# Latents, recurrence queries, first output and the queries of two head pairs turned by VectorE in 32x32 blocks and through DRAM

## The reference

```
h = rms_norm(x);  p = h @ W_in            # columns: hq hf hi hg (1024 each), c_q 512, c_kv 512, k_rope 64
o_A: 8 heads, gated linear recurrence:    # q = silu(hq), f = lb + (1-lb) sigmoid(hf), k = 1-f, v = hi
     S_t = diag(f_t) S_(t-1) + k_t v_t^T,  o_t = S_t^T q_t;  o_A = rms_norm(o) * silu(hg)
o_B: 8 heads, latent attention:           # q = rms_norm(c_q) @ w_uq,  k, v = rms_norm(c_kv) @ w_ukv
     head norms and rotary tail on q and k, softmax over chunks of 64 up to the query's, times v
x = x + concat(o_A, o_B) @ W_out
x = x + (silu(gate) * up) @ w_down        # gate, up = rms_norm(x) @ w_gate_up, width 5632
```

## Time and profile before

| | |
|---|---|
| median of 3 runs | 1124.82 us (1124.74 to 1125.54) |
| the profiled execution's own time | 1124.67 us |
| its span, first to last instruction | 1122.9 us |
| TensorE matmuls busy | 1113.2 us, 99% |
| VectorE busy | 886.8 us, 79% |
| ScalarE busy | 640.5 us, 57% |
| GpSimd busy | 51.1 us, 5% |
| moved by DMA | 228.99 MB, mean 204 GB/s |
| granted clock | 1.00 |

### The profile page before, as it was taken

How to read it: one execution, slowest core, us unless ns; L and a number is a source line. 1 busy time by engine, 2 the same in 40 slices (tenths; PEclk the granted TensorE clock), 3 DMA queues, 4 the chain that set the end, 5 groups by cost and what they waited for, 6 DMA issues and landing times.

```text
span 1122.9 us, 15465 instructions
## 1 busy us (share of the span) xinstructions
PE 1113.2 (99%) x5265; PEld 937.8 (84%) x5265; DVE 886.8 (79%) x1198; ACT 640.5 (57%) x907; POOL 51.1 (5%) x134
## 2 busy tenths in 40 slices
PE   7999999999999999999999999999999999999998
PEld 7988888888888888888888888888888888888887
DVE  5578786587876667688888888888988879889777
ACT  7566776668664556454554554554554555555553
POOL 3000000000000000000000000000000010000000
PEclk9999999999999999999999999999999999999999
DMA  8666455545555455667777677777777686666655
GB/s 267 192 196 189 158 159 156 164 141 170 197 177 168 153 187 169 212 212 234 225 229 237 222 232 238 222 229 236 224 235 226 224 276 217 207 206 199 211 190 169
DMA packets 107239, 228.99 MB, mean 204 GB/s; under 512 B 8201, under 2 KB 19250, under 8 KB 106930
## 3 DMA queue, kind: packets, MB, share of 16 engines
q1 hardware_dynamic: 101346, 209.30, 58.9%
q0 software_dynamic: 5536, 18.88, 5.8%
q10 hardware_dynamic: 304, 0.14, 0.0%
HBM read 218.32 MB, written 9.96 MB: 203 GB/s over the span
## 4 chain that ended last, share of the span: by engine, by line
PE 97%; DVE 2%; DMA 1%; ACT 0%; issue 0%; SPq 0%; DVEq 0%; ACTq 0%
PE side L1919 25%; PE main L1693 22%; PE side L1921 12%; PE main L1696 11%; PE side L1891 4%; PE side L1892 4%; PE side L1893 4%; PE main L1893 3%; PE main L1891 3%; PE main L1892 3%; PE side L1817 1%; PE side L1716 1%; DMA raw<-in_w_in 1%; PE side L1764 0%; PE side L1765 0%; DVE w_lo L1084 0%
## 5 line engine op out<-in xcount | busy, mean ns | idle before, releaser
L977 ACT CAST w_hi<-raw 128x1024 fp32r<-128x1024 f32 (+1 forms) x245 | 241.6, 990 | 172.2 <-PE side L1919 104.9
L1532 DVE TENSOR_TENSOR w_lo<-raw,w_hi 128x1024 fp32r<-128x1024 f32 (+1 forms) x245 | 275.4, 1139 | 21.9 <-ACT w_hi L977 21.6
L1084 DVE TENSOR_TENSOR w_lo<-raw,w_hi 128x1024 fp32r<-128x1024 f32 (+3 forms) x156 | 178.5, 1154 | 107.9 <-ACT w_hi L757 105.6
L757 ACT CAST w_hi<-raw 128x1024 fp32r<-128x1024 f32 (+3 forms) x156 | 153.7, 993 | 142.5 <-PE main L1693 137.6
L1693 PE MATMUL main<-w_hi,hT_hi 128*128 128x512 f32 (+2 forms) x448 | 173.4, 388 | 1.7 <-DVE hT_lo L1105 1.4
L1696 PE MATMUL main<-w_hi,hT_lo 128*128 128x512 f32 (+2 forms) x448 | 169.1, 378 | 0.0
L1921 PE MATMUL side<-w_hi,hT_lo 128*128 128x512 f32 x400 | 155.6, 389 | 0.0
L1919 PE MATMUL side<-w_hi,hT_hi 128*128 128x512 f32 x400 | 155.6, 389 | 0.0
L1693 PE MATMUL main<-w_lo,hT_hi 128*128 128x512 f32 (+2 forms) x448 | 114.6, 377 | 0.0
L1919 PE MATMUL side<-w_lo,hT_hi 128*128 128x512 f32 x400 | 106.9, 389 | 0.0
L1693 PEld LDWEIGHTS main<-w_hi,hT_hi 128*128 128x128 f32 x448 | 84.7, 189 | 15.5 <-DVE hT_lo L1105 1.8
(11 more groups left out here) (279 smaller groups left out, 1819.0 us busy)
## 6 DMA issues: line engine op xcount, KB each, us to landing
raw<-in_w_gate_up SPq DMA_DIRECT2D x176, 512.0 KB, 4.8
raw<-in_w_down SPq DMA_DIRECT2D x88, 512.0 KB, 4.5
raw<-in_w_in SPq DMA_DIRECT2D x64, 512.0 KB, 3.8
raw<-in_w_out SPq DMA_DIRECT2D x32, 512.0 KB, 3.7
raw<-in_w_in SPq DMA_DIRECT2D x15, 384.0 KB, 4.5
squares<-hiddenT POOLq DMA_DIRECT2D x11, 512.0 KB, 5.0
hiddenT<-squares POOLq DMA_DIRECT2D x44, 128.0 KB, 5.3
raw<-in_w_ukv SPq DMA_DIRECT2D x8, 512.0 KB, 3.9
```

The lines of the kernel that those rows point to most:

```text
L757: copy(w_hi[:, slot, 0:n], raw[:, slot, 0:n]).then_inc(s_hi, 1)
L977: copy(w_hi[:, n % RING, 0:cols], src).then_inc(s_hi, 1)
L1084: tt(w_lo[:, slot, 0:n], raw[:, slot, 0:n], w_hi[:, slot, 0:n].bitcast(F32), ALU.subtract)\
L1532: tt(w_lo[:, n % RING, 0:cols], src, w_hi[:, n % RING, 0:cols].bitcast(F32), ALU.subtract)\
```

## The change

Latents 0 and 1, the recurrence's queries of both halves, the first half's output, and the attention's queries of head pairs 0 and 1 are no longer turned by TensorE. A new step `swap` has VectorE transpose the tile in 32x32 blocks into a buffer; GpSimd writes that to a new DRAM tensor `swapped`, waits until it is there, and reads it back in four pieces; the steps `lat_t`, `turn` g 0, `o_t` 0 and `q_t` 0 and 1 remain, without TensorE's part, and take their values from the buffer in SBUF. Buffers are tiles that are idle at that time, and two new ones.

The positions: `swap` of the latents 19 and 27, of hq 34 and 74, of q 36 and 56, of the first output 81. `lat_t` goes from 22 (both) to 30 and 31, and from 30 (both) to 36 and 37; `q_t` 0 and 1 from 39 and 59 to 47 and 67; `turn` 0 0 stays at 45, `turn` 1 0 goes from 89 to 83; `turn` g 1 and `o_t` 0 (95) stay. On VectorE `swap` q j comes behind `q_b` j, `swap` hq 0 behind `kr_b`, `swap` hq 1 behind `q_b` 2, and `swap` o behind `o_b` 0.

```diff
+MOVED_HEADS = 2
 def schedule():
     for i in range(2):
         e = END[("lat", i + 1)]
-        s += [(e + 1, ("lat_a", i)), (e + 2, ("lat_b", i))] + [(e + 5, ("lat_t", i, n)) for n in range(2)]
+        s += [(e + 1, ("lat_a", i)), (e + 2, ("lat_b", i)), (e + 2, ("swap", "lat", i))]
+        s += [(e + 13 - 2 * i + n, ("lat_t", i, n)) for n in range(2)]
...
-        s += [(q - early, ("q_a", j)), (q - 1 if early else q + 1, ("q_b", j)), (q + 4, ("q_t", j))]
+        s += [(q - early, ("q_a", j)), (q - 1 if early else q + 1, ("q_b", j))]
+        s += [(q + 1, ("swap", "q", j)), (q + 12, ("q_t", j))] if j < MOVED_HEADS else [(q + 4, ("q_t", j))]
...
-        s += [(e + 2 + 2 * g + n * (1 + g), ("turn", g, n, t)) for n in range(2) for t in range(NT)]
+        s += [(END[("hq", g)] + 1, ("swap", "hq", g))]
+        s += [(e + 2 - 4 * g, ("turn", g, 0, t)) for t in range(NT)] + [(e + 3 + 3 * g, ("turn", g, 1, t)) for t in range(NT)]
...
-        s += [(p, ("o_a", g)), (p + 1, ("o_b", g))]
+        s += [(p, ("o_a", g)), (p + 1, ("o_b", g))] + [(p + 1, ("swap", "o", g))] * (g == 0)
...
+        hq_turned = mb("hq_turned", [P, P // Q, SEQ])
+        heads = mb("heads", [P, P // Q, NT * 2 * Q + NT * Q])
+        swap_of = {("lat", 0): hbT[:, :, :], ("lat", 1): hkT[:, :, :], ("o", 0): hgate.rearrange("p t (a c) -> p (t a) c", a=2)}
+        for j in range(MOVED_HEADS):
+            swap_of[("q", j)] = heads[:, :, :]
+        swap_of[("hq", 0)] = E[:, 0, :].rearrange("p (a c) -> p a c", a=P // Q)
+        swap_of[("hq", 1)] = hq_turned[:, :, :]
...
+            def swap(*key):
+                n, at = SWAP[key], swap_of[key]
+                wide = at.shape[2]
+                pool.wait_ge(s_swap, n + 1)
+                pool.dma_start(swapped[n, :, :, :, 0:wide].rearrange("a c b x -> (a c) b x"), at).then_inc(s_parked, 16)
+                pool.wait_ge(s_parked, 16 * (n + 1))
+                for b in range(P // Q):
+                    pool.dma_start(at[Q * b:Q * (b + 1), :, :], swapped[n, :, :, b, 0:wide].rearrange("a c x -> c a x"))\
+                        .then_inc(s_landed, 16)
+            swap("lat", 0)
+            swap("lat", 1)
+            swap("hq", 0)
+            for j in range(MOVED_HEADS):
+                swap("q", j)
             pool.wait_ge(s_lbused, 1)
             pool.wait_ge(s_side, USE[("join8", 0)] + 1)
             pool.dma_start(lb[:, :, :], hgrn_lb[:, GW:2 * GW].partition_broadcast(P)).then_inc(s_lbin, 16)
+            swap("hq", 1)
+            swap("o", 0)
...
+            def landed(*key):
+                act.wait_ge(s_landed, MOVED * (SWAP[key] + 1))
                 elif kind == "lat_t":
-                    split_hi([(mT_hi[:, k + n, :], ps[:, n * SEQ:(n + 1) * SEQ], col + n) for n in range(2)])
+                    landed("lat", i)
+                    split_hi([(by_quarter(mT_hi[:, k + n, :]), swapped_tile(("lat", i), 2 * j + n), col + n)
+                              for n in range(2)])
                 elif kind in ("q_t", "k_t"):
+                    if kind == "q_t" and j < MOVED_HEADS:
+                        landed(*key)
+                        for h in range(2):
+                            copy(by_quarter(plain[:, 2 * j + h, :]), straight[:, :, h, :, :])
+                        for h in range(2):
+                            part = slice(h * ROPE, (h + 1) * ROPE)
+                            ins = copy(by_quarter(qTr[part, j % 2, h, :]), turned[part, :, :, :])
+                        ins.then_inc(s_heads, 1)
+                        return
...
-                dve.wait_ge(s_tlo, SPLIT[s] + 1)
-                dve.sem_inc(s_given["dve"], 1)
+                if side_uses(s):
+                    dve.wait_ge(s_tlo, SPLIT[s] + 1)
+                    dve.sem_inc(s_given["dve"], 1)
+            def swap(key, src):
+                nc.vector.transpose(swap_of[key].rearrange("p b (n r) -> p n b r", r=Q),
+                                    src.rearrange("p t (k b c) -> p (t k) b c", b=P // Q, c=Q)).then_inc(s_swap, 1)
                 elif kind == "lat_t":
-                    split_lo(s, [(mT_lo[:, k + n, :], ps[:, n * SEQ:(n + 1) * SEQ], mT_hi[:, k + n, :], col + n)
-                                 for n in range(2)])
+                    split_lo(s, [(by_quarter(mT_lo[:, k + n, :])[:, t, :, :], swapped_tile(("lat", i), 2 * j + n)[:, t, :, :],
+                                  by_quarter(mT_hi[:, k + n, :])[:, t, :, :], col + n) for n in range(2) for t in range(NT)])
+                elif kind == "swap":
...
+                    elif what == "q":
+                        dve.wait_ge(s_stage, 2 * i + 1)
+                        if i:
+                            dve.wait_ge(s_heads, i)
...
+                    elif what == "hq":
+                        b = BLOCK_OF[a]
+                        dve.wait_ge(s_taken[b % 2], taken(b))
+                        swap(a, hq[:, :, :])
+                    else:
+                        dve.wait_ge(s_given["dve"], GIVEN[USE[("o_a", i, NT - 1)]])
+                        swap(a, E[:, 0, :].rearrange("p (t c) -> p t c", t=NT))
...
-                elif kind == "lat_t":
-                    i, j = a
-                    pe.wait_ge(s_lat, NT * (i + 1))
-                    turn_x(s, 2 * j, latents[i])
-                elif kind in ("q_t", "k_t"):
+                elif kind == "k_t" or kind == "q_t" and a[0] >= MOVED_HEADS:
...
                 elif kind == "scores":
                     given(("k_t", h // 2, 1))
+                    if h // 2 < MOVED_HEADS:
+                        pe.wait_ge(s_heads, h // 2 + 1)
...
-                elif kind == "turn":
+                elif kind == "turn" and a[1]:
...
-                elif kind == "o_t":
+                elif kind == "o_t" and a[0]:
```

More of the change, by code:

```diff
@@ L327 @@
 SPLIT = {step: n for n, step in enumerate(SPLITS)}
+SWAPS = [step[1:] for _, step in SCHEDULE if step[0] == "swap"]
+SWAP = {key: n for n, key in enumerate(SWAPS)}
 RMS = [step for _, step in SCHEDULE if step[0] in ("r1a", "lat_a", "q_a", "k_a", "o_a", "r2a")]
@@ L891, in step @@
                                "hg": (hgate, ACT.Silu)}[kind]
-                    if kind == "hq" and not a[0]:
-                        act.wait_ge(s_side, USE[("lat_t", 0, 1)] + 1)
+                    if kind == "hq":
+                        act.wait_ge(s_swap, SWAP[("hq", 0) if a[0] else ("lat", 0)] + 1)
                     if a[0] and kind == "hg":
-                        act.wait_ge(s_given["dve"], GIVEN[USE[("o_a", 0, NT - 1)]])
+                        act.wait_ge(s_tlo, SPLIT[("o_t", 0, 1)] + 1)
                     for t in range(NT):
@@ L902, in step @@
                         act.wait_ge(s_join, g)
-                    src = filled(s)[:, :].rearrange("p (h t) -> p h t", h=GH)
                     if n == 0:
-                        copy(hqT[:, :, t * P:(t + 1) * P], src).then_inc(s_given["act"], 1)
-                    else:
+                        landed("hq", g)
+                        src = swap_of[("hq", g)].rearrange("p a (t h r) -> p t h a r", t=NT, r=Q)[:, t, :, :, :]
+                        copy(hqT[:, :, t * P:(t + 1) * P].rearrange("p h (a r) -> p h a r", r=Q), src)
+                    else:
+                        src = filled(s)[:, :].rearrange("p (h t) -> p h t", h=GH)
+                        if not g and t == 0:
+                            act.wait_ge(s_tlo, SPLIT[("lat_t", 1, 1)] + 1)
                         activation(hkT[:, :, t * P:(t + 1) * P], src, ACT.Copy, scale=-1.0, bias=1.0)
@@ L946, in step @@
                     g, j = a
-                    dst, k = (hT_hi, 12 + 2 * j) if g else (mT_hi, MT[HEADS + 2 * j])
-                    split_hi([(dst[:, k:k + 2, :], filled(s)[:, :].rearrange("p (k t) -> p k t", k=2), V_HG)])
+                    if not g:
+                        landed("o", g)
+                        split_hi([(by_quarter(mT_hi[:, MT[HEADS + 2 * j + n], :]), swapped_tile(("o", g), 2 * j + n), V_HG)
+                                  for n in range(2)])
+                        return
+                    k = 12 + 2 * j
+                    split_hi([(hT_hi[:, k:k + 2, :], filled(s)[:, :].rearrange("p (k t) -> p k t", k=2), V_HG)])
                 elif kind == "sq2":
@@ L1246, in step @@
                     reciprocal((kind[0] + "_a",) + a, inv[:, 0:4], 4)
-                    if j:
+                    if kind == "q_b" and 0 < j <= MOVED_HEADS:
+                        dve.wait_ge(s_swap, SWAP[("q", j - 1)] + 1)
+                    elif j:
                         dve.wait_ge(s_side, USE[(kind[0] + "_t", j - 1, 1)] + 1)
@@ L1408, in step @@
                     g, j = a
-                    hi, lo, k = (hT_hi, hT_lo, 12 + 2 * j) if g else (mT_hi, mT_lo, MT[HEADS + 2 * j])
-                    split_lo(s, [(lo[:, k:k + 2, :], filled(s)[:, :].rearrange("p (k t) -> p k t", k=2),
-                                  hi[:, k:k + 2, :], V_HG)])
+                    if not g:
```

(18 more changed lines are left out.)

33 lines of the change are left out of this document (27 added, 6 removed).

## The result

Five runs of the changed kernel took 1130.85 us in the median (1130.01 to 1131.42), five of the kernel before 1124.82 (1124.74 to 1125.54): a ratio of 1.0051, with a 95% interval of 1.0039 to 1.0064. The change costs 6 us where I had forecast none. The profiled execution of the changed kernel took 1131.42 us, its span is 1129.2.

The account below looks back on a forecast made before the run. TensorE, busy 1113.2 of 1122.9 us, was taken to bound the kernel. The terms -5.7 +0.7 +0.3 +2.0 +1.1 +1.2 gave -0.4 us, a forecast of 1124.4 us, range 1121.0 to 1127.8.

Parts of the forecast that it names:

- Stages 36 to 42: 0.3 us: VectorE's added work makes low halves late at granules 40 and 42: 0.2 and 0.1 us, bounds 0 and 1.5.
- Stages 43 to 52: 2.0 us: First pairs: query copies make ScalarE's chain 1.1 us later, TensorE reaches the wait 0.87 earlier; 2.0 us, bounds 1.0 and 2.8.
- Landings cost nothing: Moves through DRAM: landings cost nothing unless they take 1.5 times what they take later in this kernel.
- It is wrong if ScalarE waits for weights: Sign against the forecast: ScalarE waiting for weights or landings; no wait of ScalarE for DMA was expected.
- The rival of the slow weight loads: Transfers slow the weight loads, weighed between granules 78 and 82: 0.6 us for each of seven moves, 1128.6 us; chance 0.10.
- Stages 31 to 33: 0.7 us: TensorE waits before granule 33 for the first latents' late second split: 0.7 us, bounds 0.2 and 1.4.
- Stages 74 to 88: 1.1 and 1.2 us: Block transposes at 74 and 81 delay the first output's product by 1.1 us in all and granule 88 by 1.2.
- The 0.87 each of stages 89 and 95 is kept.: Gain from transposes removed at stages 89 and 95 stays; granule 90 was ready 1.5 us ahead, pairs of 99 0.9.
- What TensorE loses: 5.7 us: 52 transposes removed from TensorE at 0.109 us each are worth 5.7 us, bounds 5.2 to 5.9.
- The rival of landings held up through GpSimd: GpSimd's issues held up while VectorE is busy, ScalarE waits for landings: some 1 us at three places, 1127.4; chance 0.02.

Follow-up runs that it names:

- the latents back: Changed kernel with the latents' 16 transposes back on TensorE at their old stages, the five other moves kept: 1130.13 us, ratio 1.0046 to the kernel before.
- the waits filled: Changed kernel with 22 extra transposes on TensorE before each of two waits (granule 33, first scores): 1130.97 us, ratio 1.0054 to the kernel before.
- the second form of the combined run: Kernel before plus VectorE's block transposes and the seven moves on otherwise unused tiles, each move started as its block transpose ends: 1129.84 us, ratio 1.0036.
- way of the first queries out: Changed kernel without the way through DRAM for the first pair's queries alone, the six other moves kept: 1130.13 us, ratio 1.0042 to the kernel before.

## Why the prediction was wrong

The prediction's steps give -0.3 us at the first pairs (30 transposes gone, 3.3, and 0.7, 0.3 and 2.0 added). Measured is +4.7 there. From the first pairs to granule 136 they give -0.1; measured is +1.4.

- **The step that failed is "Stages 36 to 42: 0.3 us" with "Stages 43 to 52: 2.0 us".** It followed VectorE's lateness to the low halves of granules 40 and 42, found 2.8 us of room against TensorE, and stopped there. But VectorE's low half also frees the slot for the next load, and that load ends at ScalarE's convert four granules on. VectorE's converts of 43 and 46 were 4.9 and 4.2 us later than in the kernel before, the convert of 46 on ScalarE 3.5 (0.4 of each is from the start of the execution), and behind it stands the sigmoid. The room was measured against the wrong reader. ScalarE's converts of 45 and 46 show it; in the kernel before, the wait in front of each is 1.67 us and ends with TensorE (L1693):

```profile
112.03 1.06 ACT L802 CAST w_hi<-raw 128x1024 fp32r<-128x1024 f32 x1 [2.80 <-DMA raw<-in_w_in]
114.75 1.05 ACT L802 CAST w_hi<-raw 128x1024 fp32r<-128x1024 f32 x1 [1.67 <-DMA raw<-in_w_in]
```

- **The 5.0 us at the first pairs**, by the runs: 3.1 are the ways through DRAM (4.7 less 1.6), where the prediction had none in its sum; 1.5 is the place of the query copies (1.6 less 0.1), where it had 1.1; the rest, 0.1 measured where the other steps give -1.4, is that this chain did not become earlier as TensorE did. The prediction let it move forward with the transposes that were gone; VectorE's added work took that back.
- **The two loads.** "Landings cost nothing" was right: ScalarE waits for no landing. "It is wrong if ScalarE waits for weights" came true: from 45 us to the end of this stage it waits 10.0 us in seven waits for them, and in the kernel before not once. The rival of the slow weight loads had the mechanism, at 0.10, and looked for it in the wrong place: it weighed the load between 78 and 82, and ScalarE waits for weights there only at the convert of 83, for 0.26 us. The loads that count are those of 30, 45 and 46; for the last two the share of DMA from 85 to 110 us (0.65 in the earlier trace rows) was to be read.
- **Stages 31 to 33: 0.7 us.** The mechanism was right, the size was 2.6. With the way of the first latents left out the wait is 0.81, so the rest of it, 1.8 us, comes from that way, beside which the load of granule 30 takes 8.9 us instead of 5.4; the angles behind it start 1.3 us later than in the kernel before. What the wait cost in the end is next to nothing: filling the wait gave nothing, and with the latents back, the wait gone too, 0.7 us came back.
- **Stages 74 to 88: 1.1 and 1.2 us.** These were right. From granule 60 to 88 the net lateness rises by 2.4 us (3.8 to 6.2).
- **"The 0.87 each of stages 89 and 95 is kept."** Not at 89. Granule 89 writes the banks that VectorE's norm of the last queries reads, and in the kernel before the eight transposes stood inside that wait. The last row of VectorE's norm ends at 272.48, and TensorE goes on at 272.59:

```profile
271.09 1.39 DVE L1351 SCALAR_TENSOR_TENSOR stage<-main,stat,qw_row 128x192 f32<-128x192 f32 x4
```

  The profile calls that wait "issue"; in the run with the waits filled it names VectorE's norm as what ended it:

```profile
272.59 0.50 PE L1840 MATMUL main<-w_hi,hT_hi 128*128 128x512 f32 x1 [1.10 <-DVE stage L1385]
```

  I had looked for TensorE's room in the low halves and the side banks, and not in the main banks. The net lateness at granule 89 is 0.4 more than at 88, instead of 0.87 less.
- **What TensorE loses: 5.7 us.** The spacing of 0.109 us is right: where eight had stood, at positions 22, 30 and 95, TensorE came 0.9 to 1.0 us earlier, and at 59, where six had stood, 0.7. But it is a price of TensorE's time, and only 1.9 of 4.1 us reached the end even with nothing added.
- **The rival of landings held up through GpSimd** stays unsupported, as the prediction had it: GpSimd's issues beside a VectorE that is busy 23.16 of 25 us (from 85 to 110, the second row here) took what they take elsewhere (0.55 us in the earlier trace rows). No run here shows the rule of the Trainium skill ("SBUF — State Buffer", SBUF: two separate sides) at work. The tile's instructions (ns min/median/max, first and last start):

```profile
L734 POOL DMA_DIRECT2D hkT<-swapped x4: 551/551/558, 77.9 to 79.6; - x4
L734 POOL DMA_DIRECT2D E<-swapped x4: 551/551/558, 98.8 to 100.5; - x4
```

Left open: why the same traffic cost 2.9 us net in the change and 0.7 to 0.9 in the second form of the combined run (2.7 and 1.6 to 2.0 by the medians). It is argued, not shown, that the moment decides: in the change TensorE is a microsecond earlier by then, so the load of granule 30 is issued in the middle of the four returning pieces (8.9 us), there behind most of them (6.9). Some 0.4 us that the change loses at granule 99, in every run where the first output is split from SBUF, was not looked into either.

## What to carry to other kernels

Before work is moved off the busiest engine, remove it there and add nothing: that one run bounds the gain (here 1.9 of 4.1 us), since an engine that is busy 99% can still be paced at a few places by others. Measure the room of an added instruction against everyone who waits for its engine, and above all against the slot that its engine frees for the next load; a chain of slot, load and convert carries a delay past the granules that looked safe. A wait of the busiest engine, and a half clock behind it, can cost nothing, as here, if a later wait is set by another chain; the chain of waits shows which it is.

## What the hardware showed that was not expected

- A load of 512 KB took 8.9 us when it was issued within the 1.7 us in which four pieces of 128 KB came back from DRAM, 5.5 us without them, and 7.1 beside a move of 384 KB.
- TensorE's granted clock stood at 0.50 for some 3 us after waits of 2.60 and 2.15 us, and at 1.00 after waits of 2.27 to 2.71 us in five other runs. With 22 transposes in each of the two waits it was 1.00. The half clock cost nothing at the end.
- Reading SBUF in four pieces of 128x128, VectorE's split takes 1.05 to 1.14 us for two tiles, where two pieces from PSUM took 0.87; the prediction had 0.8. A block transpose of 128x512 takes 0.71 us.
- Some executions of the kernels here, the one before too, are 1.5 to 2 us longer than the median. Two such executions were profiled (way of the first queries out, and the second form of block transposes and traffic): TensorE came 2.1 and 1.9 us later to granule 15 than in the profile of the kernel before (the other runs: 0.6 earlier to 0.5 later), and its granted clock stood at 0.50 for some 3 us from 17 us on, behind waits of 1.92 and 1.81 us. In the other fifteen profiled runs it is 1.00 there, after waits of up to 1.89 us.
